# Norm statistics on four columns and spread back by matmuls, the modulation scale in VectorE's step, weight roundings moved round the root

## What is computed

```python
def rms_norm(t, w):
    y = tf * lax.rsqrt(jnp.mean(tf * tf, axis=-1, keepdims=True) + NORM_EPS)
    return (y * w).astype(t.dtype)

def modulate(h, shift, scale):
    return h * (1.0 + scale[:, None, :]) + shift[:, None, :]
```

## Time and profile before

| | |
|---|---|
| median of 3 runs | 4033.93 us (4023.92 to 4040.32) |
| profiled execution | 4035.21 us, of which 4033.4 us are the span from the first to the last instruction |
| mean granted clock of TensorE | 0.938 of full speed |
| TensorE busy | 3567.5 us, 88% of the span, 12706 matmul records |
| VectorE busy | 1873.4 us, 46% |
| ScalarE busy | 1103.7 us, 27%; 125 table loads, 160.4 us |
| GpSimd busy | 111.7 us, 3% |
| DMA | 89 GB/s over the span; a weight chunk of 512 KB lands 3.6 us after its issue (median) |

### The profile page before, as it was taken

How to read it: one execution, slowest core, us unless ns; L and a number is a source line. 1 busy time by engine, 2 the same in 40 slices (tenths; PEclk the granted TensorE clock), 3 DMA queues, 4 the chain that set the end, 5 groups by cost and what they waited for, 6 DMA issues and landing times. The chain is left out here.

```text
span 4033.4 us, 36059 instructions
## 1 busy us (share of the span) xinstructions
PE 3567.5 (88%) x12706; PEld 2407.5 (60%) x12706; DVE 1873.4 (46%) x2537; ACT 1103.7 (27%) x1425; POOL 111.7 (3%) x204
## 2 busy tenths in 40 slices
PE   4997789999689999867999997999979679989987
PEld 1444468877358877633788643588847346558433
DVE  5856256536358835142664297466233433153001
ACT  1221243323432213321453201344142222132000
POOL 0000000000000000000000300000000000000000
PEclk9896999999899999978999998999989889999988
DMA  5231146522035522201233210233322112223111
GB/s 215 99 120 54 42 148 196 190 89 73 11 110 192 195 86 84 63 0 52 80 97 94 73 52 32 78 96 94 97 94 84 32 52 84 83 68 98 48 62 62
DMA packets 100408, 360.87 MB, mean 89 GB/s; under 512 B 11152, under 2 KB 11168, under 8 KB 100064
## 3 DMA queue, kind: packets, MB, share of 16 engines
q1 hardware_dynamic: 77936, 276.07, 21.5%
q0 software_dynamic: 20080, 75.27, 5.8%
q10 hardware_dynamic: 2304, 8.39, 0.5%
HBM read 357.59 MB, written 2.10 MB: 89 GB/s over the span
## 5 line engine op out<-in xcount | busy, mean ns | idle before, releaser
L1613 DVE TENSOR_TENSOR weight_lo<-weight_ring,weight_hi 128x1024 fp32r<-128x1024 f32 (+1 forms) x390 | 468.6, 1203 | 930.0 <-ACT weight_hi L1124 926.2
L1124 ACT ACTIVATE weight_hi<-weight_ring 128x1024 fp32r<-128x1024 f32 (+1 forms) x390 | 406.3, 1043 | 1266.2 <-PE proj_banks L688 927.6
L688 PE MATMUL proj_banks<-h_hi,weight_hi 128*128 128x512 f32 x1584 | 617.3, 390 | 9.6 <-DVE weight_lo L1613 9.6
L688 PE MATMUL proj_banks<-h_hi,weight_lo 128*128 128x512 f32 x1584 | 617.0, 390 | 0.0
L688 PE MATMUL proj_banks<-h_lo,weight_hi 128*128 128x512 f32 x1584 | 616.8, 389 | 0.0
L1647 DVE RECIPROCAL scratch<-scratch 128x512 f32<-128x512 f32 (+1 forms) x39 | 129.2, 3312 | 479.4 <-ACT scratch L1124 479.3
L688 PEld LDWEIGHTS proj_banks<-h_hi,weight_hi 128*128 128x128 f32 x1584 | 297.7, 188 | 73.4 <-issue 11.6
L688 PEld LDWEIGHTS proj_banks<-h_hi,weight_lo 128*128 128x128 f32 x1584 | 297.6, 188 | 62.2
L688 PEld LDWEIGHTS proj_banks<-h_lo,weight_hi 128*128 128x128 f32 x1584 | 297.7, 188 | 61.4
L645 PE MATMUL proj_banks<-scratch,weight_ring 128*128 128x512 f32 x640 | 293.5, 622 | 27.5 <-DMA weight_ring<-in_w_dnr 27.5
L688 PE MATMUL proj_banks<-mid_hi,weight_hi 128*128 128x512 f32 x704 | 275.3, 391 | 7.3 <-DVE weight_lo L1613 7.3
(11 more groups left out here) (259 smaller groups left out, 4378.6 us busy)
## 6 DMA issues: line engine op xcount, KB each, us to landing
weight_ring<-in_w_up SPq DMA_DIRECT2D x176, 512.0 KB, 3.6
ada_ring<-in_ada POOLq DMA_DIRECT2D x96, 512.0 KB, 3.9
weight_ring<-in_w_dn SPq DMA_DIRECT2D x64, 512.0 KB, 3.5
weight_ring<-in_w_br SPq DMA_DIRECT2D x32, 512.0 KB, 3.7
weight_ring<-in_w_upr SPq DMA_DIRECT2D x32, 512.0 KB, 3.6
weight_ring<-in_w_dnr SPq DMA_DIRECT2D x32, 512.0 KB, 4.5
scratch<-in_ada POOLq DMA_DIRECT2D x24, 512.0 KB, 4.3
weight_ring<-in_w_dn SPq DMA_DIRECT2D x32, 384.0 KB, 3.1
```

The source lines that it names most:

```text
L688: last = mm(proj.banks[:, u % RING, :], stationary(split0 + n)[:, w], moving(k), start=k + m == 0, stop=k == kt - 1 and m == 2)
L1124: return nc.scalar.activation(out, in_, func, **kw)
L1613: return v.tensor_tensor(out, a, b, op)
```

## The change

- `norm` of TensorE: instead of eight ones-matmuls of 512 columns, the squares are the stationary side. VectorE adds the squared tiles 0 to 6 into one (`sum_up`, six additions of 128x512, those of norms 1 to 8 inside `residual`); four matmuls with one column of ones each take that sum, four more the eighth tile, into four columns of a bank: token 128j+p lies in column j, partition p.
- Root and reciprocal are taken on these 128x4 values (`STD`, `INV` in `small`, which grows from 160 to 192 columns). Four matmuls spread each column over 128 rows (the column, repeated, as stationary side, the unit matrix moving) into a new bank `("bc", r)`, from which VectorE reads it directly.
- A root of one value stands before the last square of every norm.
- In modulated norms VectorE applies the gain in its own step; ScalarE adds only the shift, and in split norms writes the rounded `h_hi` in that same pass. `h_lo` is H plus shift minus `h_hi`.
- The second weight chunk of the projection behind is rounded, and its rest taken, after the root and the reciprocal instead of before.
- `round_down` is gone: in norms behind a feed-forward, ScalarE rounds three chunks, then squares one tile, in turn.
- `first_pair` takes the low parts tile by tile for both banks, so both are full at the end.

```diff
@@ first_pair (TensorE)
-        for t in range(2):
-            for k in range(KD):
-                if t == 0:
-                    pe.wait_ge(s["h_ready"], h_count(r, k))
+        for k in range(KD):
+            pe.wait_ge(s["h_ready"], h_count(r, k))
+            for t in range(2):
                 last = mm(proj.bank((name, t)), c.hi(split0 + t)[:, k * P:(k + 1) * P], lo(k), start=False, stop=k == KD - 1)
-            last.then_inc(proj.full_sem, 1)
+                if k == KD - 1:
+                    last.then_inc(proj.full_sem, 1)
@@ norm (TensorE)
-        sum_squares(("ss", r), lambda k: (s["sq_ready"], 8 * r + k + 1), lambda k: T(squares_at(r) + k), KD)
+        bank = open_bank(mix, ("ss", r))
+        for half, (sem, n) in enumerate(((s["sq_summed"], 6 * (r + 1)), (s["sq_ready"], 8 * (r + 1)))):
+            pe.wait_ge(sem, n)
+            for j in range(NB):
+                squares = T(squares_at(r) + (KD - 1 if half else 0))
+                last = mm(bank[:, j:j + 1], squares[:, j * P:(j + 1) * P], c.square("ones")[:, 0:1], start=half + j == 0, stop=half + j == NB,
+                          skip_group_check=True)
+        last.then_inc(mix.full_sem, 1)
+        bank = open_bank(mix, ("bc", r))
+        pe.wait_ge(s["rstd_ready"], r + 1)
+        for j in range(NB):
+            last = mm(bank[:, j * P:(j + 1) * P], c.small[:, INV + j:INV + j + 1].broadcast_to([P, P]), c.square("ident"), start=True, stop=True)
+        last.then_inc(mix.full_sem, 1)
@@ norm (ScalarE)
             elif r in NORM_AFTER:
-                act.wait_ge(*proj.emptied((NORM_AFTER[r], k)))
+                stage = NORM_AFTER[r]
+                if stage in SPLIT:
+                    for n in range(3 * k + SPLIT_RING, min(3 * k + 3 + SPLIT_RING, 3 * KD - 1)):
+                        round_chunk(stage, n)
+                act.wait_ge(*proj.emptied((stage, k)))
...
             st.done(f(T(squares_at(r) + k), X(k), ACT.Square), s["sq_ready"])
-            if r in SPLIT_UP and k == KD - 2:
-                up = SPLIT_UP[r]
-                for n in range(SPLIT_RING):
-                    round_chunk(up, n)
-        root(("ss", r), T(RSTD), D)
+            if k == KD - 2:
+                st.link(f(c.small[:, STD:STD + 1], eps, ACT.Sqrt))
+                if NORM_AFTER.get(r) in SPLIT:
+                    round_chunk(NORM_AFTER[r], 3 * KD - 1)
+                if r in SPLIT_UP:
+                    round_chunk(SPLIT_UP[r], 0)
+        act.wait_ge(*mix.filled(("ss", r)))
+        ins = f(c.small[:, STD:STD + NB], mix.bank(("ss", r))[:, 0:NB], ACT.Sqrt, scale=1.0 / D, bias=eps)
+        ins.then_inc(mix.emptied(("ss", r))[0], 1)
+        if r in SPLIT_UP:
+            round_chunk(SPLIT_UP[r], 1)
...
-                ins = f(H(k), H(k), ACT.Identity, scale=c.g(use, k), bias=c.m(layer, part, k))
-                ins.then_inc(s["h_raw"] if r in SPLIT_NORMS else s["h_ready"], 1)
                 if r in SPLIT_NORMS:
-                    round_h(r, k)
+                    st.done(f(c.norm_hi(r, k), H(k), ACT.Identity, bias=c.m(layer, part, k)), s["h_rounded"])
+                else:
+                    f(H(k), H(k), ACT.Identity, bias=c.m(layer, part, k)).then_inc(s["h_ready"], 1)
@@ norm (VectorE)
+    def sum_up(r, k):
+        total = T(squares_at(r))
+        dve.wait_ge(s["sq_ready"], 8 * r + k + 1)
+        st.done(tt(total, total, T(squares_at(r) + k), ALU.add), s["sq_summed"])
+
     def norm(r):
+        if r not in NORM_AFTER:
+            for k in range(1, KD - 1):
+                sum_up(r, k)
         if r in SPLIT_UP:
-            for n in range(SPLIT_RING):
-                rest_chunk(SPLIT_UP[r], n)
-        inverse(("ss", r), T(RSTD))
+            rest_chunk(SPLIT_UP[r], 0)
+        dve.wait_ge(*mix.emptied(("ss", r)))
+        st.done(v.reciprocal(small[:, INV:INV + NB], small[:, STD:STD + NB]), s["rstd_ready"])
+        if r in SPLIT_UP:
+            rest_chunk(SPLIT_UP[r], 1)
+        dve.wait_ge(*mix.filled(("bc", r)))
+        rstd = mix.bank(("bc", r))
         for k in range(KD):
             if r in MODULATED:
-                st.done(tt(H(k), X(k), T(RSTD), ALU.mult), s["xn_ready"])
+                ins = stt(H(k), X(k), c.g(MODULATED[r][0], k), rstd, ALU.mult, ALU.mult)
+                st.done(ins, s["xn_ready"])
...
+                if r in MODULATED:
+                    use, layer, part, _ = MODULATED[r]
+                    ins = stt(c.norm_lo(r, k), H(k), c.m(layer, part, k), hi, ALU.add, ALU.subtract)
+                else:
+                    ins = tt(c.norm_lo(r, k), H(k), hi, ALU.subtract)
@@ residual (VectorE)
+            if k >= 2:
+                sum_up(after, k - 1)
             dve.wait_ge(*proj.filled(key))
```

More of the change, by code:

```diff
@@ L210, in mixing_keys @@
 def mixing_keys():
-    k = [("ss", 0)]
+    k = [("ss", 0), ("bc", 0)]
     k += [("rot_i", t) for t in range(5)]
@@ L228, in mixing_keys @@
         k += [("av", *units[n - 2])] if n >= 2 else []
-    k += [("ss", 1), ("ss", 2)]
+    k += [("ss", 1), ("bc", 1), ("ss", 2), ("bc", 2)]
     k += [("stat_s", t) for t in range(8)] + [("pool", g) for g in range(4)]
@@ L234, in mixing_keys @@
         k += [("sb", h - 2)] if h >= 2 else []
-    k += [("ss", 3), ("ss", 4)]
+    k += [("ss", 3), ("bc", 3), ("ss", 4), ("bc", 4)]
     k += [("acol", 0)]
@@ L241, in mixing_keys @@
         k += [("mn", h, 0), ("mn", h, 1), ("md", h), ("stat_m", h)]
-    k += [("ss", 5), ("ss", 6), *(("dw", t) for t in range(KD)), ("lnm", 0), ("lnv", 0), ("ss", 7), ("ss", 8), ("ssc", 0), ("ss", 9)]
+    k += [("ss", 5), ("bc", 5), ("ss", 6), ("bc", 6), *(("dw", t) for t in range(KD)), ("lnm", 0), ("lnv", 0), ("ss", 7), ("bc", 7), ("ss", 8), ("bc", 8), ("ssc", 0)]
+    k += [("ss", 9), ("bc", 9)]
     k += [("rot_r", t) for t in range(8)]
@@ L247, in mixing_keys @@
     k += [("sgu", t) for t in range(2)]
-    k += [("ssy", 0), ("ss", 10), ("ssy", 1)]
+    k += [("ssy", 0), ("ss", 10), ("bc", 10), ("ssy", 1)]
     return k
@@ L305, in __init__ @@
         self.acc = sb("ada_acc", [P, 8])
-        self.small = sb("small", [P, 160])
+        self.small = sb("small", [P, 192])
         with ExitStack() as mixing:
@@ L455 @@
 PLAIN = {4: ("norm_mix_2", 0), 5: ("norm_ffn_2", 0), 6: ("norm_mix_2", 8), 7: ("norm_ffn_2", 8), 8: ("norm_final_2", 0)}
+PLAIN_SPLIT = (4, 5, 7)
 SQ0, RSTD = 44, 54
+STD, INV = 160, 164
 def squares_at(norm):
@@ L1137, in round_h @@
     def round_h(r, k):
-        n = 8 * SPLIT_NORMS.index(r) + k + 1
-        act.wait_ge(s["h_raw"], n)
+        act.wait_ge(s["h_raw"], 8 * PLAIN_SPLIT.index(r) + k + 1)
         st.done(f(c.norm_hi(r, k), H(k), ACT.Copy), s["h_rounded"])
@@ L1159, in round_ahead @@
         st_round(f(c.hi(split), c.slot(chunk), ACT.Copy))
-    def round_down(layer):
-        for n in range(SPLIT_RING, 3 * KD):
-            round_chunk(f"dn{layer}", n)
     def norm(r):
@@ L1428, in conv_ffn @@
                 f(T(52 + 2 * p), T(52 + 2 * p), ACT.Silu).then_inc(s["conv_act"], 1)
-        round_down(layer)
     norm(5)
@@ L1659, in norm @@
                 out = X(k) if r == 8 else H(k)
-                ins = stt(out, X(k), c.v(name, at + k), T(RSTD), ALU.mult, ALU.mult)
+                ins = stt(out, X(k), c.v(name, at + k), rstd, ALU.mult, ALU.mult)
                 if r == 8:
@@ L1663, in norm @@
                 elif r in SPLIT_NORMS:
-                    ins.then_inc(s["h_raw"], 1)
+                    st.done(ins, s["h_raw"])
                 else:
@@ L1667, in norm @@
                     dve.wait_ge(s["h_ready"], h_count(r, k))
+        dve.sem_inc(*mix_release(mix, ("bc", r)))
         if r in SPLIT_NORMS:
@@ L1695, in residual @@
     def residual(stage, gate=None, bias=None):
+        after = [r for r in NORM_AFTER if NORM_AFTER[r] == stage][0]
         for k in range(KD):
```

6 lines of the change are left out of this document (3 added, 3 removed).

## The result

The changed kernel takes **4041.6 us** (median of 8 runs, 4037.4 to 4050.2), the kernel before 4033.9 (8 runs beside them, 4023.9 to 4040.3): a ratio of 1.0019, 95% interval 1.0010 to 1.0027. That is no change by the bound of the prediction, and 57 us from the 3985 forecast. The profiled run took 4040.36 us.

What follows compares the result with a forecast made beforehand. TensorE is busy 88%; gains lie in its idle stretches and ones-matmuls at eleven norms. These sum to 54.0 us, less 5 for the clock: 49, from 4035.21 to 3986.2, predicted 3985; range 3975 to 3995, with other cases 3966 to 4004.

Steps and rivals of the forecast that it cites:

- what is hidden: Work claimed not to delay TensorE: rests and sums in down projections (1.0 us of slack), queues, and moved buffers, costed at nothing.
- norm 1: First h_hi matmul 7.4 us earlier, pair closing 10 us earlier, gap behind it 3.7 instead of 2.05: 8.3 us won.
- norms 4 and 5: Norms without modulation, where TensorE already set the pace behind the start: 4.9 and 4.0 us won.
- Norms 0, 9 and 10: First loses 3.7 us, no residual hiding its sums; second wins 5.0 before the context's projection; last loses 0.6.
- both halves: In norm 0, the two groups of one-column matmuls that sum the squares, 2.4 us together.
- Norm 8: The load of `dist` is issued when this norm's statistic is full, and the context norm awaits its landing: 4.2 us won.
- The charge for the clock: Behind the gaps of norms 1, 5 and 7, eight slow matmuls each, 1.65 us, three times: 5 us lost.
- The clock stays up: Rival: short bursts through the norms hold TensorE at 2.4 GHz, so pairs start fast: 3970 us; chance 0.22.
- All small steps at their upper bounds: Rival: 0.24 us a record in the norms' small matmuls and a clock fall behind all seven pairs: 4001 us; chance 0.15.
- Slower by tiny matmuls that don't overlap: Rival: the norms' tiny matmuls don't overlap their weight loads, 0.6 us a record: 4069 us; chance 0.03.
- It doesn't do what it says: Rival: sums delay residuals and weight rests; TensorE waits for `weight_lo` about 1 us in 32 down-projection tiles: 4017 us; chance 0.05.
- higher price of a PSUM source: VectorE's products reading the broadcast bank: 0.065 us more on each of 88, 5.7 us by the skill; not charged.

Runs made afterwards that it cites:

- moved_on: The changed kernel with 224 instead of 192 columns in `small`, so every buffer behind lies another 128 bytes on: 3993.96 us, ratio 0.9899 to the kernel before.
- no_sums: The changed kernel with 224 columns in `small` and, in norms 0 and 10, no sums on VectorE: 3982.39 us, ratio 0.9858 to the kernel before.

## Why the prediction was wrong, point by point

**The step that failed** stands in the part on what is hidden: "Scratch of 192 instead of 160 columns moves later buffers by 128 bytes; I cost it at nothing, no row shows a buffer's place to matter." It costs 51.8 us in the kernel before and 47.6 in the changed one. That no row shows an effect was no reason for nothing: every row had been taken at one place. Other terms without a row got bounds from both sides, and this one did not. A bound was at hand: 9,168 rounded products each start some 227 ns after the one ahead, so each per cent on them is 21 us.

**What of the rest held.** moved_on is the change at an undisturbed place, so its trace tests the terms. Us from the last product of the stage ahead to the third weight tile (norms 6 and 0: to the first product), before less moved_on, the forecast in brackets: norm 1 8.4 (8.3), norm 2 7.7 (8.4), norm 3 10.7 (10.3), norm 4 3.9 (4.9), norm 5 3.1 (4.0), norm 7 5.5 (5.7), norm 6 6.9 (7.5). Norms 0, 8, 9 and 10: -5.8 (-3.7), -1.1 (4.2; to the context's first product), 5.6 (5.0; from there to the end of the products with norm 9's result), -2.2 (-0.6). Sum 43 instead of 54; less the clock's 5 this makes 38, where the two spans differ by 41.3. Two terms explain most of the 11 us; of the rest, norms 4 and 5 won about 1 us less each than forecast.

*Norms 0, 9 and 10 run at the low clock.* The prediction put both halves at 2.4 us. Timeline of norm 0, after:

```profile
64.02 3.55 PE L763 MATMUL mix_banks<-squares,scratch 128*128 128x1 f32 x16 [64.02 <-DVE scratch L1633]
67.66 0.26 ACT L1142 ACTIVATE small<-mix_banks,others 128x4 f32<-128x4 f32 x1 [11.18 <-PE mix_banks L763]
68.03 0.18 DVE L1682 RECIPROCAL small<-small 128x4 f32<-128x4 f32 x1 [4.16 <-ACT small L1142]
...
68.35 2.05 PE L769 MATMUL mix_banks<-squares,small 128*128 128x128 f32 x8 [0.79 <-DVE small L1682]
...
72.24 2.04 PE L630 MATMUL proj_banks<-h_tiles,weight_ring 128*128 128x512 f32 x2 [1.83 <-ACT h_tiles L1142]
```

0.22 us a record instead of 0.12, and the broadcast is on the path, with no weight chunk to hide it: 72.2 instead of 70.3. (The prediction's own terms for norm 0 add up to 70.1, and those for norm 1 give 7.5 us where it writes 7.4; both are slips of no weight.) The column of the clock shows 1.00 here; but the trace's first entry on the clock lies only at 76 us, and the durations don't agree with the column. In norm 10 they are the same and the column shows the low level:

```profile
3555.00:3558.60 3.60, 3.53 (x16) 3.49 (x16) 1.19 (x1) 0.00 (x0) 0.00 (x0) 0.50 0.30 67
```

*Norm 8 was to win as much as the load of `dist` is issued earlier.* Against the last product ahead it is issued 4.3 us earlier, and lands only 1.8 earlier. The list of DMA issues, KB and us from issue to landing; before:

```profile
scratch<-in_dist POOLq DMA_DIRECT2D x1, 1536.0 KB, 6.7
```

After:

```profile
scratch<-in_dist POOLq DMA_DIRECT2D x1, 1536.0 KB, 9.2
```

Two loads issued just ahead in the same queue didn't move, and an earlier issue only waited longer: likely behind them, which no run tested. Norm 9's halves at the low clock then stand ahead of the context's projection, and norm 8 comes out even.

*The charge for the clock* had the right number of falls, and that was in part luck. Windows behind the gaps of norms 1, 2, 3, 5 and 7, after:

```profile
532.50:536.50 4.00, 4.00 (x12) 3.14 (x13) 3.25 (x5) 1.45 (x2) 0.53 (x1) 0.64 0.63 159
914.00:918.00 4.00, 3.97 (x17) 3.28 (x18) 3.79 (x8) 0.62 (x2) 0.00 (x0) 1.00 0.41 131
1163.00:1167.00 4.00, 4.00 (x18) 3.26 (x19) 3.84 (x6) 0.00 (x0) 0.53 (x1) 1.00 0.78 261
...
1924.40:1928.40 4.00, 3.97 (x9) 3.18 (x10) 3.58 (x5) 2.82 (x4) 0.00 (x0) 0.50 0.52 138
2573.50:2577.50 4.00, 4.00 (x12) 3.21 (x13) 3.58 (x5) 2.77 (x4) 0.00 (x0) 0.66 0.54 139
```

Behind the three gaps of 3.62 us the granted clock is 0.50 to 0.66, behind those of 2.3 to 2.5 us it stays at 1.00. The Trainium skill ("TensorE: Matmul & The Clock Gate", HAM oscillation) has idle between bursts sending TensorE back to half rate; the trace shows this for the longer gaps and not for the shorter, so in this run the charge for three pairs, not for seven, fits. But the length of the gap does not decide it. Windows of moved_on, behind the gaps of norms 4 (2.48 us) and 7 (3.64 us):

```profile
1535.30:1539.30 4.00, 4.00 (x11) 3.18 (x12) 3.86 (x6) 2.78 (x4) 0.00 (x0) 0.60 0.39 131
...
2547.40:2551.40 4.00, 4.00 (x18) 3.32 (x19) 3.58 (x5) 2.73 (x4) 0.00 (x0) 1.00 0.50 139
```

Over the ten traces with the interleaved low parts the clock falls behind 27 of the 30 gaps of 3.6 us and behind 11 of the 40 of 2.3 to 2.9 us; over the other four traces, behind both gaps of 2.6 to 2.7 us and behind 3 of the 26 of at most 2.1 us, each time norm 5's. The longer gaps fell more often, but no length decides. The trace of before, from which the prediction took its rule, had shown one draw for each pair. It also left out a gain: the fall behind norm 3's gap in before (0.61 in the earlier trace rows) is gone in the changed kernel (1.00 in the window at 1163.00), which brings the 38 us above to about 40.

**The rivals.** *The clock stays up* (0.22): no; all seven pairs still start at 0.50, as in norm 1, after:

```profile
515.40:519.40 4.00, 4.00 (x10) 3.13 (x11) 3.82 (x6) 3.69 (x6) 0.00 (x0) 0.50 0.35 120
```

*All small steps at their upper bounds* (0.15): in part. A record takes 0.22 at the low clock, near the bound of 0.24, but only in norms 0, 9 and 10, where TensorE had been idle for 17 us or more; in norm 1 it takes 0.12. *Slower by tiny matmuls that don't overlap* (0.03): no, 0.12 to 0.22 us is far from 0.42. *It doesn't do what it says* (0.05): no; in the down projections the first of the three products waits 6.7 us in all for weight_lo, and 7.3 before. What rose are the gaps behind the pairs, by 1.6 us at six of the seven. None of the rivals was the mechanism that decided; the side they left open was a cost in the stages that are not edited. The Trainium skill's higher price of a PSUM source ("VectorE: DVE Perf Modes", The TRN2 errata) is not seen here either: the 48 modulated products that read the broadcast bank take 747 ns on average, as those of the earlier trace rows without PSUM.

## What to carry to other kernels

When a kernel streams thousands of matmuls back to back, compare their mean duration and their count in a fixed window, before and after an edit, ahead of anything else: an edit that grows one small buffer can shift all those behind it, and a per cent on such a stream outweighs every wait removed elsewhere. Where rounded products bind, lay weights and moving operands (all parts of both) at places alike in 256 bytes, and let a small buffer grow by whole multiples of 256 bytes. This is tried here for products with the weights loaded and h streaming. A cost that no row shows is a cost to bound, by what a small slowing of the largest group would make, and not a nothing.

## What the runs showed that was not expected

- After a rounded product of 128x512 starts, the next one starts 226.8 ns later if its moving operand lies alike in 256 bytes with its own weights and with those loaded beside it, and 232 to 235 ns later otherwise; 32, 64 and 128 bytes apart are much the same, and moving both sides together changes nothing. This is shown for the products with the weights loaded (8,688 of 9,168) and not for the others. Plain float32 products (429.2 ns a record, two records a product) don't feel it. Loads of weights last 188 to 189 ns in either case. Why is open: the runs show which pairs of operands matter, not the circuit.
- The Trainium skill ("SBUF — State Buffer", SBUF: two separate sides) has TensorE never waiting on anyone at SBUF. It also gives weight loads a second, independent read port ("SBUF — State Buffer", A bandwidth-pool intuition that's wrong). No run here was made to test another engine's effect; but here the placement of one of TensorE's two operands against the other costs 2.6% of the spacing, so the two are not independent in time.
- In no_sums 64 one-column records kept TensorE's loads busy for 13.78 us, from 50.7 to 64.5 us, at nearly twice the time that a record has at full clock. In norm 10 of that run the granted clock reads 0.50 over the 16 us that hold the same 64 records.
- The granted clock's column can read 1.00 near the start of a program, ahead of the first entry on the clock, while the durations are those of the low level.
